# A two-block transformer kernel on one core: first projection in a new order, first norm weights on another queue with ten idle transposes, and more weight slots for the experts

## The reference

```
h = rms_norm(x, norm_mix_pre)            # first block
q, k, v, u, gates = split(h @ w_in)
y_a = chunk_band_attention(q, k, v) @ w_attn_out
y_b = multiscale_pool(u) @ w_pool_out
x += rms_norm((g_a * y_a + g_b * y_b) @ w_o)
x += rms_norm(conv_gated_ffn(rms_norm(x)))
...                                      # second block: two more attentions, then
h = h + hier_moe(rms_norm_2(h, g_ffn), w_rg, w_re, w1, w3, w2)
...                                      # in hier_moe, for each of 32 experts
hdn = silu(xb @ w1[e]) * (xb @ w3[e])
ys = hdn @ w2[e]
```

## Time and profile before

| | |
|---|---|
| median of 3 runs | 1580.75 us (1577.08 to 1580.89) |
| profiled execution, its own time | 1578.17 us |
| its span, first to last instruction | 1576.2 us |
| TensorE busy | 1524.8 us, 97% of the span |
| VectorE, ScalarE, GpSimd busy | 46%, 34%, 11% |
| transfers | 311.22 MB, 197 GB/s over the span |
| mean granted TensorE clock | 0.996 |

### The profile page before, as it was taken

One profiled execution on the slowest core, in us unless ns is written; L12 is line 12 of the kernel. 1 busy time (PEld: TensorE's weight loads), 2 busy tenths in 40 slices (PEclk: granted clock), 3 DMA queues, 4 the chain that ended last, 5 costly groups with the idle time before them and its releaser, 6 DMA issues.

```text
span 1576.2 us, 19637 instructions
## 1 busy us (share of the span) xinstructions
PE 1524.8 (97%) x7802; PEld 1064.8 (68%) x7802; DVE 717.6 (46%) x1208; ACT 530.1 (34%) x910; POOL 165.8 (11%) x172
## 2 busy tenths in 40 slices
PE   5999999999999999999999989999999999999898
PEld 5776788888888888888777766745444444444367
DVE  5345432464444544478665787631122132132174
ACT  4334322354332422345355577421100011010042
POOL 1014100002111111111300210020000000000000
PEclk9999999999999999999999999999999999999999
DMA  7111422312222222222110232879999999999951
GB/s 275 41 67 61 174 80 107 121 67 87 102 107 104 91 89 91 107 94 83 53 53 28 95 121 94 334 270 406 421 421 421 421 421 421 420 420 419 421 239 55
DMA packets 45437, 311.22 MB, mean 197 GB/s; under 512 B 5136, under 2 KB 5648, under 8 KB 10016
## 3 DMA queue, kind: packets, MB, share of 16 engines
q1 hardware_dynamic: 42336, 296.22, 47.1%
q0 software_dynamic: 3008, 13.72, 2.4%
HBM read 301.52 MB, written 8.39 MB: 197 GB/s over the span
## 4 chain that ended last, share of the span: by engine, by line
PE 88%; DVE 5%; ACT 3%; DMA 2%; issue 2%; DVEq 0%; ACTq 0%; POOLq 0%
PE bank L795 21%; PE bank L2487 14%; PE bank L1413 7%; PE bank L2503 6%; PE bank L839 6%; PE bank L2470 4%; PE bank L2520 4%; PE bank L856 4%; PE bank L2686 3%; PE bank L1270 3%; PE bank L808 2%; PE bank L827 2%; DMA M<-in_w 2%; PE bank L874 1%; PE bank L848 1%
## 5 line engine op out<-in xcount | busy, mean ns | idle before, releaser
L619 DVE TENSOR_TENSOR w_lo<-M,w_hi 128x2048 fp32r<-128x2048 f32 x73 | 169.8, 2332 | 183.0 <-ACT w_hi L614 183.0
L2487 PE MATMUL bank<-M 128*64 128x512 f32 x1024 | 228.9, 599 | 2.8 <-DMA M<-in_w 2.8
L614 ACT ACTIVATE w_hi<-M 128x2048 fp32r<-128x2048 f32 x73 | 139.1, 1912 | 148.4 <-PE bank L795 56.9
L795 PE MATMUL bank<-HTH,w_hi 128*128 128x512 f32 x432 | 168.1, 389 | 0.0
L795 PE MATMUL bank<-HTL,w_hi 128*128 128x512 f32 x432 | 168.1, 389 | 0.0
L795 PE MATMUL bank<-HTH,w_lo 128*128 128x512 f32 x432 | 168.0, 389 | 0.0
L2487 PEld LDWEIGHTS bank<-M 128*64 128x64 f32 x1024 | 71.7, 137 | 139.3 <-issue 138.2
L2503 PE MATMUL bank<-M 128*64 128x512 f32 x512 | 114.0, 595 | 1.5 <-DMA M<-in_w 1.5
L2645 DVE TENSOR_TENSOR X<-bank,X 128x512 f32<-128x512 f32 x69 | 46.6, 689 | 114.7 <-PE bank L2520 114.6
L795 PEld LDWEIGHTS bank<-HTL,w_hi 128*128 128x128 f32 x432 | 81.1, 188 | 16.9
L795 PEld LDWEIGHTS bank<-HTH,w_lo 128*128 128x128 f32 x432 | 81.1, 188 | 16.8
(11 more groups left out here) (371 smaller groups left out, 2860.3 us busy)
## 6 DMA issues: line engine op xcount, KB each, us to landing
M<-in_w SPq DMA_DIRECT2D x192, 1024.0 KB, 10.1
M<-in_wd SPq DMA_DIRECT2D x78, 1024.0 KB, 4.8
M<-in_nb SPq DMA_DIRECT2D x4, 1536.0 KB, 6.8
X<-in_x SPq DMA_DIRECT2D x4, 512.0 KB, 10.1
M<-in_rows POOLq DMA_DIRECT2D x4, 512.0 KB, 6.4
M<-in_tb POOLq DMA_DIRECT2D x8, 256.0 KB, 4.2
rowb<-in_rows POOLq DMA_DIRECT2D x4, 512.0 KB, 5.5
xs_parts<-XSH POOLq DMA_DIRECT2D x1, 2048.0 KB, 11.1
```

The source lines that it names most:

```text
L614: e.activation(hi[:, :], slots[slot_of[n]], ACT.Copy).then_inc(split_hi_done, 1)
L619: e.tensor_tensor(lo[:, :], slots[slot_of[n]], hi[:, :], ALU.subtract).then_inc(split_lo_done, 1)
L795: m = e.matmul(out[:, :], w[:, k0 + k, n0:n0 + 128], v[k], start=(k == 0 and i == 0), stop=(k == len(hi) - 1 and i == 2))
L2487: m = e.matmul(b[64 * s:64 * s + 64, :], Xe[:, 4 * kh + k, o + C * s:o + C * s + C], unit_w(key, 4)[:, k, :], start=(kh == 0 and k == 0), ...
```

## The change

It has three parts.

1. **Order of the first projection.** `proj_pe` goes by operand: in each half first the 16 high-high matmuls of q and k, then the 16 with the low activations, then the 16 with the low weights. The first kind needs only the ACT results (`n_hi`, `split_hi_done`), the second also HTL of the half's two blocks, the third the low weights. Blocks 2 and 3 are transposed behind the second and the third kind of the first half. The counts are the same.
2. **Norm weights and idle transposes.** The load of the first norm weights moves from POOL to SP, directly behind x block 0 and ahead of the first constants, with a semaphore of its own, and ten transposes of the identity into the bank of q stand behind the transposes of block 1.
3. **Slots of the experts.** A slot 12 (`SPARE_SLOT`, area 30784) is added that is free from the beginning, so the unit behind the dense ones can be loaded without a wait. `HD` and `hT` move to 28736 and 29760, and slot 7 is now given back. So 13 units can be loaded ahead, and 9 slots turn over. The room comes from a smaller `st` and from a smaller scratch area for the descriptors of POOL's transfers (1024 bytes for each partition in place of the default 16384); `PH`, `PL` and `TMP` of the last stage get other places.

```diff
@@ first loads, SP and POOL
             for t in range(TT):
                 e.dma_start(X[:, t, :], x_d[t * 128:(t + 1) * 128, :]).then_inc(d_x[t], 16)
                 if t == 0:
+                    load_gain(e, 0)
                     e.dma_start(cst[:, 0:NFIRST], cst_d[:, 0:NFIRST]).then_inc(d_ident, 16)
...
         def first_loads_pool(e):
-            load_gain(e, 0)
             e.wait_ge(d_x[TT - 1], 16)
@@ pre_pe
             norm_pe(e, 0, 0)
             norm_pe(e, 0, 1)
-
+            idle_bank = bank[ps.at["q", 0][0]]
+            for n in range(10):
+                e.transpose(idle_bank[:, 0:128], ident, ident)
@@ proj_pe
-            split_ready(e, ("in", 0))
             outs = [claim(e, (name, 0)) for name in ("q", "k")]
+            wh, wl = parts(("in", 0), KD)
             for half in range(2):
                 ts = slice(half * 256, (half + 1) * 256)
-                ht_ready(e, 0, 2 * half)
-                ht_ready(e, 0, 2 * half + 1)
-                for j, (b, fills) in enumerate(outs):
-                    m = gemm3_T_some(e, ("in", 0), b, j, ts)
-                    if half:
-                        m.then_inc(fills, 1)
-                    elif j == 0:
-                        norm_pe(e, 0, 2)
-                        norm_pe(e, 0, 3)
+                high_ready(e, ("in", 0))
+                e.wait_ge(n_hi, 4 * half + 4)
+                for i, (w, src) in enumerate(((wh, HTH), (wh, HTL), (wl, HTH))):
+                    if i == 1:
+                        ht_ready(e, 0, 2 * half)
+                        ht_ready(e, 0, 2 * half + 1)
+                    if i == 2:
+                        split_ready(e, ("in", 0))
+                    for j, (b, fills) in enumerate(outs):
+                        for k in range(KD):
+                            m = e.matmul(b[:, ts], w[:, k, j * 128:(j + 1) * 128], src[:, k, ts], start=(i == k == 0),
+                                         stop=(i == 2 and k == KD - 1))
+                        if half and i == 2:
+                            m.then_inc(fills, 1)
+                    if half == 0 and i:
+                        norm_pe(e, 0, i + 1)
@@ slots
-        slots += [area(o, UNIT) for o in (20480, 13312, 24576, 13312 + UNIT, 13312 + 2 * UNIT)]
+        slots += [area(o, UNIT) for o in (20480, 13312, 24576, 13312 + UNIT, 13312 + 2 * UNIT, 30784)]
...
-        open_slots = deque([(slot_of[n], n) for n in (NDENSE - 2, NDENSE - 1)] + [(i, "nbr") for i in (2, 3, 9, 11, 6)]
+        open_slots = deque([(SPARE_SLOT, "free")] + [(slot_of[n], n) for n in (NDENSE - 2, NDENSE - 1)] + [(i, "nbr") for i in (2, 3, 9, 11, 6)]
...
-            if slot_of[n] < NS_MOE:
+            if slot_of[n] not in ONCE:
                 open_slots.append((slot_of[n], n))
...
-        HD = [area(20480 + 512 * i, 512) for i in range(2)]
-        hT = [area(21504 + 512 * i, 512) for i in range(2)]
+        HD = [area(28736 + 512 * i, 512) for i in range(2)]
+        hT = [area(29760 + 512 * i, 512) for i in range(2)]
...
-    nc = bacc.Bacc("TRN2", target_bir_lowering=False, num_devices=1)
+    nc = bacc.Bacc("TRN2", target_bir_lowering=False, num_devices=1, dynamic_dma_scratch_size=1024)
```

More of the change, by code:

```diff
@@ L21 @@
 NSPLIT = 3
-M_SZ = 43072
+M_SZ = 47168
 SPLIT0 = NS * UNIT
@@ L29 @@
 NS_ONCE = 5
+ONCE = range(NS_MOE + 1, NS_MOE + NS_ONCE)
+SPARE_SLOT = NS_MOE + NS_ONCE
 NE = 32
@@ L145, in build @@
         wpg = sb("wpg", [128, 4, 128])
-        st = sb("st", [128, 1760])
+        st = sb("st", [128, 1536])
         nex_i = sb("nex_i", [1, 1], I32)
@@ L168, in build @@
         YH, YL = ([overlay(f"{n}{i}", A0 + 13312 + o + 2048 * i, D) for i in range(3)] for n, o in (("YH", 0), ("YL", 1024)))
-        PH = [overlay(f"PH{i}", A0 + o, UNIT) for i, o in enumerate((0, 2048, 4096, 19456))]
-        PL = [overlay(f"PL{i}", UNIT * i, UNIT) for i in range(NS_MOE)]
+        PH = [overlay(f"PH{i}", A0 + o, UNIT) for i, o in enumerate((0, 2048, 4096, 28736))]
+        PL = {i: overlay(f"PL{i}", UNIT * i, UNIT) for i in range(NS_MOE)}
+        PL[NS_MOE], PL[SPARE_SLOT] = overlay("PL_low", A0 + 20480, UNIT), overlay("PL_spare", A0 + 30784, UNIT)
         OS = overlay("OS", A0 + 19968, TT, C)
@@ L213, in stat @@
             o_st[0] += n
-            assert o_st[0] <= 1760
+            assert o_st[0] <= 1536
             return a
@@ L219, in build @@
         out_of = [sem(f"out_of{i}") for i in range(8)]
-        w_ready = [sem(f"w_ready{i}") for i in range(NS_MOE + NS_ONCE)]
+        w_ready = [sem(f"w_ready{i}") for i in range(SPARE_SLOT + 1)]
         w_used, split_hi_done, split_lo_done = sem("w_used"), sem("split_hi_done"), sem("split_lo_done")
@@ L515, in build @@
         A_TWO, TWO = unit["ap", 1], unit["in2", 9]
-        rounds = [0] * (NS_MOE + NS_ONCE)
+        rounds = [0] * (SPARE_SLOT + 1)
         slot_of, slot_round, slot_after, last_in = {}, {}, {}, {}
@@ L655, in load_gain @@
             o = BIG[GAIN_OF[R]]
-            e.dma_start(GAIN[R][:, :], rows_d[:, o:o + D].to_broadcast([128, D])).then_inc(d_gain, 16)
+            e.dma_start(GAIN[R][:, :], rows_d[:, o:o + D].to_broadcast([128, D])).then_inc(d_gain if R else d_gain_first, 16)
         def norm_act(e, R, t, s):
@@ L687, in norm_dve @@
                 dve_own.mark(e.reciprocal(r, sq))
-                e.wait_ge(d_gain, 16 * (R + 1))
+                e.wait_ge(*((d_gain, 16 * R) if R else (d_gain_first, 16)))
                 if t >= 2 and R == 1:
@@ L811, in gemm3_T_part @@
                     m.then_inc(fills, 1)
[L813 to L820, removed]
         def gemm_tok_part(e, key, j, t, out, low):
@@ L2231, in expert_loads @@
                     filled(e, ("o2", 3, 1))
+                elif before == "free":
+                    pass
                 elif before < NDENSE:
@@ L2677, in moe_pool @@
                         load_gain(e, 4)
-        TMP = [area(o, 512) for o in (21504, 22016, 28224)]
+        TMP = [area(o, 512) for o in (19456, 19968, 28224)]
         def gate_part(e, out, n, t, ks, x, low, start=False, stop=False, cs=slice(0, 512)):
@@ L2755, in gains @@
             def gains(t):
-                e.wait_ge(d_gain, 16 * 5)
+                e.wait_ge(d_gain, 16 * 4)
                 if t == 3:
```

2 lines of the change are left out of this document (1 added, 1 removed).

## The result

| | before | changed |
|---|---|---|
| median of 5 runs | 1578.81 us (1576.45 to 1580.89) | 1569.76 us (1567.84 to 1571.43) |
| profiled execution | 1578.17 us | 1568.23 us |
| span | 1576.2 us | 1566.4 us |
| first scores (start of the chain's 4 small matmuls) | 36.24 us | 31.52 us |
| router's first matmuls (32, 3.63 us in all) | 1013.18 us | 1008.72 us |

The ratio is 0.9941 with a 95% interval of 0.9925 to 0.9957. The forecast was 1569.5.

A forecast was written before the change was run, and what follows sets the result against it. TensorE, busy for 97% of the span, was taken to bound the kernel, with transfers equally tight in the experts. Terms 4.8 + 5.1 = 9.9 us gave 1568.3 to 1570.9, middle 1569.5 us; range 1564 to 1576.

The forecast's parts named there:

- What bounds the kernel: Whole kernel: TensorE busy 97% of the span, experts equally tight on transfers; a gain at the start goes through.
- When blocks 0 and 1 are scaled: Start: with norm weights in SP's queue, block 1 is scaled at 10.5 in place of 13.43, 2.9 us won.
- the first rival: Start: load slow in SP's queue too, or transposes don't bring the clock; 2.6 or 3.6 for 4.8 us; chance 0.18.
- The first matmul: First projection: new order waits for ACT and the ten idle transposes, so 15.4 in place of 19.66 us.
- The clock: First projection: TensorE runs without a long gap, so matmuls take 0.12 us each from the first on.
- term one: Start up to the first scores: they start at 31.4 in place of 36.24 us, 4.8 us won.
- The attention: Behind the first scores: moves as a whole, since its loads and splits hang on TensorE's own progress.
- term two: Experts: two units of lead bring transfers 5.0 us earlier, some 0.9 us of waits stay, 5.1 us won.
- Half of the lead: Experts, lower bound of term two: 2.5 us won if only one unit stays ahead.
- The descriptor area: POOL's transfers: area 16 times smaller; any wait for room would be covered by the first projection.
- lead lost: Experts: TensorE's pace sets the landing times in the last pairs, waits stay; gain 4.8 alone, 1574.5 us; chance 0.12.
- the slower one: Experts: more transfers under way cost rate; at 405 GB/s 15.4 us lost, 1585 us; chance 0.03.

The follow-up runs named there:

- e11: Changed kernel with the first constants ahead of the norm weights in SP's queue and twelve idle transposes at the very start; median 1569.41 us, ratio 0.9942.
- e2: Kernel before with new projection order, norm weights on SP and ten idle transposes, old slots and descriptor area; median 1573.97 us, ratio 0.9972.
- e7: Changed kernel with the spare slot but slot 7 not given back; span 1572.2 us, experts 520.1 us.
- e8: Changed kernel with slot 7 given back but without the slot free from the beginning; span 1570.7 us, experts 522.2 us.
- e12: Changed kernel with slot 7 given back but no free slot, the same edit profiled again and timed; median 1570.88 us, ratio 0.9954.
- e10: Changed kernel with the norm weights' load back on POOL, all else as changed; median 1570.48 us, ratio 0.9949.
- e4: Kernel before with only the norm weights' load moved to SP behind x block 0, old order, no idle transposes; first scores at 35.15 us.
- e5: Changed kernel without the ten idle transposes; first scores at 32.64 us, first 16 matmuls 3.76 us.
- e3: Kernel before with only the new order of the first projection, norm weights on POOL, no idle transposes; first scores at 32.00 us.
- e6: Changed kernel with twelve more idle transposes at the very start of TensorE's list; first scores at 31.23 us.
- e9: Kernel before, profiled once more with no edit; first scores at 34.25 us, experts 523.9 us.

## Why the prediction was right, step by step

**What bounds the kernel.** Right. What was won at the start went through the middle, and what was won in the experts went through the last stage.

**When blocks 0 and 1 are scaled** (forecast: constants at 5.9, block 1's x at 7.2, scaled from 9.2, 2.9 us won). Mis-sized. The constants landed at 6.7, ACT took up block 1 right behind block 0 at 8.1, and the scaling began at 9.95, 2.2 earlier than in the profile before. The step that failed is "I take 410 GB/s for what lies behind x block 0": from 4 to 6 us it was 223, though POOL's queue was empty. The constants are not what slowed it: in e11 they have landed at 4.4 us, and the rate from 4 to 6 is 188 GB/s, at a share of 0.49. The broadcast row was under way in each of these stretches, as the first rival had it (until 6.4 us in the changed kernel, 7.3 in e11); whether it is the cause no run separates. (The "15 now" there is a slip; the time meant is the 3.06 us.) And the base was a late one: with the load on POOL block 1 is scaled from 12.15, 11.87, 11.41, 10.38 or 10.21 (mean 11.2), with it on SP behind x from 9.92 to 10.61 (eight profiles, mean 10.1), 1.1 us earlier.

Even this 1.1 doesn't reach the scores, since block 0 sets them and not block 1, by which the prediction reckoned. Counted from the start of block 0's scaling, the scores come 23.03 to 23.05 us later in all six profiles with the new order and just the ten idle transposes, the load on SP (changed, e2, e7, e8, e12) or on POOL (e10). Block 0 is scaled from 8.27 to 10.18 with the load on POOL (five profiles, mean 9.16) and from 8.46 to 9.15 with it on SP (eight, mean 8.66): on POOL it waits for the norm weights, on SP for the constants behind them. That is 0.5 us on the average, less than it varies on POOL. In the three comparisons whose starts differ in the load's queue alone it won 0.0 (e4 against the mean of the old start), lost 0.6 (e5 against e3) and won 0.4 us (the five with the new start against e10).

**The first matmul** (forecast 15.4). Measured 15.41, and it waits for ACT, whose copy came at 15.27. The ten transposes are through at 14.6, as they ran at twice the pace that I gave them. That was luck: in e2, where they took 1.92 us, the first matmul starts at 15.41 too, but behind the transposes.

**The clock** (forecast: 0.12 us each from the first matmul on). Right, and e3, e5 and the eight profiles with the ten show it: without them the first 16 matmuls took 3.46 and 3.76 us, with them 2.14 to 2.16. They fill the gap between the transposes of block 1 and the first matmul. The Trainium skill, TensorE: Matmul & The Clock Gate, section PE-mode transpose, whose rule was the case against it, is contradicted by these float32 transposes, and the measurement decides: in e6 the pace of transposes doubled with nothing else run before.

**The first scores** (forecast 31.4, term one 4.8). Measured 31.52 and 4.7. But between the profiles with the old start (36.24, 35.02, 34.25: mean 35.2) and those with the new one (31.52, 31.54, 31.96, 31.65, 31.74: mean 31.7) it is 3.5. Counted from block 0's scaling to the scores, the old order takes 25.1 to 26.1 (mean of four profiles 25.7), the new one without idle transposes 23.7 and 24.2 (mean 23.95), with the ten 23.0. So the order gives 1.8, the transposes 0.9 (1.1 in e5 against the changed kernel) and the load 0.5, 3.2 together; the 0.3 that is left is that the norm weights happened to land later in the three profiles with the old start (block 0 scaled from 9.5) than on the average. Of the 4.7 between the two first profiles the rest, 1.5, is chance too: the kernel before began block 0's scaling at 10.18, 1.0 later than the mean on POOL, the changed one 0.2 earlier than the mean on SP, and the clock rose late in the former (0.3). So the step that failed in term one is the load, "so 2.9 us are won here": it is worth about 0.5, and the forecast of 31.4 for the changed kernel was met, while the term, taken from one late profile, was too large by 1.3 us.

**The attention** (forecast: it moves as a whole). Of 4.7 us 4.5 were left at the router. Both profiles have two slow stretches of the clock in the middle; with one or four of them the middle would have been up to 1 us shorter or 3 us longer, so one pair of profiles alone would not have shown this.

**The experts** (term two: 5.1 us; waits of 0.7 to 0.9 stay). Measured 5.3: five profiles with the old slots take 523.1 to 524.5 (mean 523.8), six with the new ones 517.6 to 518.9 (mean 518.4). Waits of 1.3 to 2.2 stay. That transfers end last is shown by where the last wait for weights ends: 484.1 to 485.4 us behind the router with the old slots, 478.6 to 479.9 with the new ones, and from there to the last stage it is 39.0 to 39.1 us in all fourteen profiles. So the landing sets the stage, and what TensorE does ahead of it costs nothing. Four of the five profiles with the old slots have a slow stretch of the clock behind their longest wait, e9 has none: it waited for 6.3 us where the first profile waited for 4.3 and lost 1.7 to the slow clock, and its stage is no shorter (523.9; the four 523.1 to 524.5). A slow stretch ahead of the last wait only shortens the waits behind it. My sum counted the 1.7 among the 6.0 us that hang on late weights. That is right as the room that the lead can fill; the slow clock is no loss beside it. The transfers had the room that was forecast: at the same distance from the router as in the earlier trace rows, from 1025.54 and from 1035.54 us, the changed kernel moves 143 and 338 GB/s in place of 133 and 295, about one unit more, the other being loaded before. No run has the moved tiles and the small descriptor area without either slot, so 5.3 is strictly the worth of the whole third part.

**Half of the lead** (bound: 2.5, if one unit stays ahead). One slot gives 3.7 (e7) or, given back later, 1.6 and 2.4 (e8, e12); together 5.3. Half of that is 2.7, and 1.4 is the scatter of the stage, so the bound of 2.5 for one unit is neither confirmed to better than 1 us nor contradicted. SP's list shows that a slot is a unit of lead: 56.3 us behind the router the kernel before has asked for its 22nd unit, counted from the one asked for 50.5 us ahead of it, e7 and e8 each for the 23rd, the changed kernel for the 24th. SP's timeline of the changed kernel shows the spare slot's unit (second row) issued right behind the last dense one, in a stretch with little else to move:

```profile
958.25 0.33 SPq L889 DMA_DIRECT2D M<-in_wd  x1
958.62 0.43 SPq L2241 DMA_DIRECT2D M<-in_wd  x1
972.42 27.88 SPq L2241 DMA_DIRECT2D M<-in_w  x8
```

Slot 7's second unit is asked for some 90 us later (e8, 1048.9 us), where the transfers soon run at 395 GB/s (e8, 1055 to 1095 us). If the late slot is really worth less, that may be why; no run here separates it.

**The descriptor area.** e2 has the large one, the changed kernel the small one: scores at 31.54 and 31.52, the middle 976.3 and 977.2. It costs nothing that can be seen.

**Sum and rivals.** 3.5 + 5.3 = 8.8; the medians differ by 9.05. The sum of 9.9 was 0.9 too large, and the base between two levels (1579.4) was 0.6 above the later median of 1578.81. The two errors cancel but for 0.3, so that the forecast of 1569.5 hit 1569.8 is in part luck. The case "load slow in SP's queue too" is half true: the load was worth little, but the rate was low only until 6 us (223 GB/s, not 164); from 6 to 8 it was 424. The transposes' half of that case fell. The case "lead lost" and the slower one (rate falls with more transfers under way) did not come: 421 GB/s again. The range of 1564 to 1576 held all five runs.

## What to carry to other kernels

A product of split operands needs its parts at different times: going by operand instead of by k lets TensorE start on the high parts while the low ones are made (1.8 us here). Ten idle transposes in the 1.9 us gap ahead of the first matmuls were worth some 1 us. Where transfers are saturated for long and end last, each slot of lead is worth about the time of one transfer (2.5 us for 1 MB here; 1.6 to 3.7 measured), once; that it takes idle time of the transfer engines earlier is argued, not shown. And a start that waits for transfers varies by 2 us in the same kernel: take its base from several profiles, compare stages, not spans, and count the stretches at half clock before an edit is credited. When a load is moved, follow the operation that the result really hangs on: here block 0's scaling, by which the move is worth 0.5 us, and not block 1's.

## What the runs showed of the hardware that was not expected

Transposes of float32 raise TensorE's clock (e6: 0.2 us and then 0.1 each in neighbouring windows, only transposes before). In groups with gaps of 1.5 and 1.1 us between them they did not for long (e11: ten still took 2.21 us, 9 us after the first), yet the 16 matmuls right behind those ten took 2.16. The granted clock falls to 0.50 for short stretches in the middle of the work, one to four times in the 970 us of the middle, at different places in profiles of the same code. The landing of the first 0.5 MB load on POOL's queue let DVE start between 8.3 and 10.2 us in five profiles with the same first loads, and at 8.4 and 10.2 in the same kernel. And with POOL's queue empty, SP's first loads still moved only 223 GB/s between 4 and 6 us, at a share of 0.86.
